# A recurrence on 64 x 64 quarters of the TensorE array

## What is computed

```
def step(S, inp):                       # for every token, every head
    r_t, w_t, k_t, v_t, kk_t, a_t = inp
    sa = jnp.einsum('bhij,bhj->bhi', S, -kk_t)
    S = S * w_t + sa[..., None] * (kk_t * a_t) + v_t[..., None] * k_t
    return S, jnp.einsum('bhij,bhj->bhi', S, r_t)
```

## Time and profile before

| | us |
|---|---|
| median of 3 runs | 1198.92 |
| range of the runs | 1193.13 to 1202.80 |
| the profiled execution | 1198.65 |
| its span | 1196.9 |
| TensorE, products, busy | 1139.4 |
| VectorE busy | 626.6 |
| ScalarE busy | 337.0 |
| recurrence, first product of round 0 | 568.11 |
| first products of rounds 1, 2 and 3 | 604.61, 636.68, 664.82 |
| last product of the inverse of round 3, start | 692.05 |

### The profile page before, as it was taken

The page is one execution under the profiler, slowest core; times in us unless marked ns, Lnnn a source line. Parts: engine busy times, 40 slices in busy tenths (PEclk is TensorE's granted clock), DMA queues, the critical chain, the costliest instruction groups (busy, mean ns, idle before and its releaser), DMA issues.

```text
span 1196.9 us, 21721 instructions
## 1 busy us (share of the span) xinstructions
PE 1139.4 (95%) x8994; PEld 1116.0 (93%) x8994; DVE 626.6 (52%) x1075; ACT 337.0 (28%) x496; POOL 40.7 (3%) x57
## 2 busy tenths in 40 slices
PE   6999999999999997999898999999999999999996
PEld 6999999999999997998787889989999999999996
DVE  5533343333345875889767616785343443344446
ACT  5321222111213433521234343442122221122221
POOL 0000000000000000210221100000000000000001
PEclk9999999999999988999799998899999999999998
DMA  6313232223222211332501002203233232323222
GB/s 223 113 55 105 89 102 74 88 88 100 76 95 79 74 50 53 77 89 76 41 1 36 1 1 73 57 33 106 80 99 104 70 105 71 106 71 105 70 71 75
DMA packets 35391, 92.23 MB, mean 77 GB/s; under 512 B 10368, under 2 KB 12928, under 8 KB 35200
## 3 DMA queue, kind: packets, MB, share of 16 engines
q1 hardware_dynamic: 34320, 88.78, 23.9%
q10 hardware_dynamic: 1008, 2.56, 0.6%
HBM read 88.05 MB, written 3.28 MB: 76 GB/s over the span
## 4 chain that ended last, share of the span: by engine, by line
PE 81%; DVE 12%; ACT 3%; issue 3%; DMA 1%; DVEq 0%; SPq 0%; ACTq 0%
PE ps L306 71%; DVE wl L289 1%; PE ps L1131 1%; DVE mixf L984 1%; PE ps L1137 1%; PE ps L1138 1%; PE ps L367 1%; DVE a L447 1%; ACT wh L284 1%; DVE tb L676 1%; PE ps L376 1%; DMA x<-in_x 1%; DVE xx L1310 1%; DVE mixf L985 1%; PE ps L1573 1%
## 5 line engine op out<-in xcount | busy, mean ns | idle before, releaser
L306 PE MATMUL ps<-xh,wh 128*128 128x272 f32 x1840 | 404.2, 293 | 22.7 <-DVE wl L289 8.8
L306 PE MATMUL ps<-xh,wl 128*128 128x272 f32 x1840 | 400.7, 291 | 0.0
L306 PE MATMUL ps<-xl,wh 128*128 128x272 f32 x1840 | 399.7, 290 | 0.0
L306 PEld LDWEIGHTS ps<-xh,wh 128*128 128x128 f32 x1840 | 299.6, 191 | 25.2 <-DVE wl L289 15.0
L306 PEld LDWEIGHTS ps<-xl,wh 128*128 128x128 f32 x1840 | 299.7, 191 | 0.0
L306 PEld LDWEIGHTS ps<-xh,wl 128*128 128x128 f32 x1840 | 297.9, 191 | 0.0
L284 ACT ACTIVATE wh<-raw 128x1024 fp32r<-128x1024 f32 (+1 forms) x163 | 167.7, 1032 | 319.5 <-PE ps L306 201.2
L289 DVE TENSOR_TENSOR wl<-raw,wh 128x1024 fp32r<-128x1024 f32 (+1 forms) x163 | 192.5, 1202 | 43.6 <-ACT wh L284 43.3
L306 PE MATMUL ps<-hh,wh 128*128 128x272 f32 x704 | 156.8, 289 | 0.0
L306 PE MATMUL ps<-hh,wl 128*128 128x272 f32 x704 | 155.8, 288 | 0.0
L306 PE MATMUL ps<-hl,wh 128*128 128x272 f32 x704 | 155.6, 288 | 0.0
(11 more groups left out here) (311 smaller groups left out, 850.5 us busy)
## 6 DMA issues: line engine op xcount, KB each, us to landing
raw<-in_w_gu SPq DMA_DIRECT2D x88, 512.0 KB, 3.7
raw<-in_w_d SPq DMA_DIRECT2D x32, 512.0 KB, 3.6
raw<-in_w_in SPq DMA_DIRECT2D x19, 512.0 KB, 3.5
raw<-in_w_d SPq DMA_DIRECT2D x16, 384.0 KB, 3.0
raw<-in_w_out SPq DMA_DIRECT2D x8, 512.0 KB, 3.6
out_y<-x SPq DMA_DIRECT2D x16, 136.0 KB, 1.7
con<-in_con ACTq DMA_DIRECT2D x1, 1158.5 KB, 5.1
x<-in_x ACTq DMA_DIRECT2D x4, 272.0 KB, 5.6
```

What stands on the lines that cost most here:

```text
L306: last = pe.matmul(out[:, n], left[:, s, j], right[:, j, n * H:n * H + H], start=first and opens and j == order[0], stop=final and closes ...
```

## The change

The inverse's matrices become 128 rows by 64 columns: the rows of chunk c keep their partitions, and the columns of both chunks share the same 64. Each 128 x 128 product of steps 2 to 12 becomes two products of 64 x 64, one for each c, on rows hp[c] and output partitions hp[c]. The transposes of step 2 become products with the identity. Line 1157 becomes two 64 x 64 products, on output partitions rows(c). The evictions of steps 2 to 12 have half the columns. VectorE's masks of step 1 are ordered anew: `nib` in two instructions of 64 partitions, one addition and one mask for both p instead of two each, `akb` in two of 64 partitions, `rbk` as before but behind both of `akb`. Step 2 waits for one count of `tt1` for both p. The mask and level tables in `con` shrink from 9 x 128 to 64 + 128 + 6 x 64 columns.

```diff
--- before.py
+++ after.py
@@ -66,7 +66,7 @@
 
 CCOL = {}
 _n = 0
-for _name, _k in (("ident", P), ("ones", P), ("hb", P), ("mask", 3 * P), ("lev", 6 * P), ("scan", N), ("cnt", 32),
+for _name, _k in (("ident", P), ("ones", P), ("hb", P), ("mask", C + P), ("lev", 6 * C), ("scan", N), ("cnt", 32),
                   ("wcol", 2), ("eps", 3), ("smask", 64), ("slev", 64), ("bsel", 8), ("idc", 64)):
     CCOL[_name] = _n
     _n += _k
@@ -88,12 +88,12 @@
     c[:, CCOL["ident"]:][:, :P] = s == t
     c[:, CCOL["ones"]:][:, :P] = 1
     c[:, CCOL["hb"]:][:, :P] = s // C == t // C
-    c[:, CCOL["mask"]:][:, :P] = (s // C == t // C) & (s < t)
-    c[:, CCOL["mask"] + P:][:, :P] = (s // C != t // C) & (s % C < t % C)
-    c[:, CCOL["mask"] + 2 * P:][:, :P] = s % C <= t % C
+    c[:, CCOL["mask"]:][:, :C] = s % C < t[:, :C]
+    c[:, CCOL["mask"] + C:][:, :P] = s % C <= t % C
     for n, b in enumerate(LEVELS):
-        near = (s // (2 * b) == t // (2 * b)) & (s // b != t // b)
-        c[:, CCOL["lev"] + n * P:][:, :P] = near & (s < t if n == 0 else s > t) | (s == t)
+        r, q = s % C, t[:, :C]
+        near = (r // (2 * b) == q // (2 * b)) & (r // b != q // b)
+        c[:, CCOL["lev"] + n * C:][:, :C] = near & (r < q if n == 0 else r > q) | (r == q)
     col = np.arange(N)
     start = np.where(col < NP_, col % C == 0, (col - NP_) % NT == 0)
     c[:, CCOL["scan"]:][:, :N] = 1 - start
@@ -201,15 +201,15 @@
 
         spots["wkv"] = W0
         bv = at("wkv", "bv", [2, 2, 3, P])
-        nib = at("wkv", "nib", [2, 2, P])
-        akb = at("wkv", "akb", [2, 2, P])
+        nib = at("wkv", "nib", [2, 2, C])
+        akb = at("wkv", "akb", [2, 2, C])
         rbk = at("wkv", "rbk", [2, 2, 2, P])
         rhs = at("wkv", "rhs", [2, P])
         assert spots["wkv"] <= LO
         spots["wkv"] = LO + 8 * N
-        tt_ = at("wkv", "tt", [2, 2, 2, P])
-        tf = at("wkv", "tf", [2, 2, P])
-        xx = at("wkv", "xx", [2, 2, P])
+        tt_ = at("wkv", "tt", [2, 2, 2, C])
+        tf = at("wkv", "tf", [2, 2, C])
+        xx = at("wkv", "xx", [2, 2, C])
         sfin = at("wkv", "sfin", [2, C])
         assert spots["wkv"] <= UB
         spots["wkv"] = UB
@@ -1121,21 +1121,27 @@
                     continue
                 elif s == 2:
                     b = job(p)
-                    pe.wait_ge(S("tt1"), 2 * t + p + 1)
+                    pe.wait_ge(S("tt1"), t + 1)
                     for h in range(2):
-                        last = pe.transpose(b[:, P * h:P * h + P], tt_[:, p, 1, h], ident)
+                        for c in range(2):
+                            last = pe.matmul(b[hp[c], C * h:C * h + C], tt_[hp[c], p, 1, h], ident[hp[c], C * c:C * c + C],
+                                             start=True, stop=True)
                 elif s % 2:
                     pe.wait_ge(S(f"r{s - 1}"), 2 * t + p + 1)
                     b = job(p)
                     for h in range(2):
-                        last = pe.matmul(b[:, P * h:P * h + P], nib[:, p, h], tt_[:, p, 0, h], start=True, stop=True)
+                        for c in range(2):
+                            last = pe.matmul(b[hp[c], C * h:C * h + C], nib[hp[c], p, h], tt_[hp[c], p, 0, h], start=True, stop=True)
                 else:
                     pe.wait_ge(S(f"r{s - 1}"), 2 * t + p + 1)
                     b = job(p)
                     for h in range(2):
                         if s < 12:
-                            pe.matmul(b[:, P * h:P * h + P], tt_[:, p, 1, h], xx[:, p, h], start=True, stop=True)
-                        last = pe.matmul(b[:, 256 + P * h:256 + P * h + P], xx[:, p, h], tt_[:, p, 1, h], start=True, stop=True)
+                            for c in range(2):
+                                pe.matmul(b[hp[c], C * h:C * h + C], tt_[hp[c], p, 1, h], xx[hp[c], p, h], start=True, stop=True)
+                        for c in range(2):
+                            last = pe.matmul(b[hp[c], P + C * h:P + C * h + C], xx[hp[c], p, h], tt_[hp[c], p, 1, h],
+                                             start=True, stop=True)
                 last.then_inc(S("job"), 1)
             if s == 1:
                 b = [job(h) for h in range(2)]
@@ -1154,8 +1160,9 @@
                     pe.wait_ge(S("r0"), 2 * t + p + 1)
                     for h in range(2):
                         k = P * p + C * h
-                        last = pe.matmul(ps[:, 4 + t % 2, k:k + C], akb[:, p, h], bv[:, t % 2, p, 2, C * h:C * h + C],
-                                         start=k == 0, stop=t == 0, skip_group_check=True)
+                        for c in range(2):
+                            last = pe.matmul(ps[rows(c), 4 + t % 2, k:k + C], akb[hp[c], p, h], bv[hp[c], t % 2, p, 2, C * h:C * h + C],
+                                             start=k == 0, stop=t == 0, skip_group_check=True)
                 if t == 0:
                     last.then_inc(S("c_injob"), 1)
 
@@ -1186,7 +1193,7 @@
                     pe.wait_ge(S("r12"), 2 * t + p + 1)
                     for h in range(2):
                         q = P * p + C * h
-                        last = pe.matmul(ps[rows(c), 4 + k, 256 + q:256 + q + C], tf[rows(c), p, h, cols(c)],
+                        last = pe.matmul(ps[rows(c), 4 + k, 256 + q:256 + q + C], tf[rows(c), p, h],
                                          rhs[rows(c), p, C * h:C * h + C], start=True, stop=True)
                 last.then_inc(S("c_ujob"), 1)
             elif hop in ("s0", "s1"):
@@ -1228,11 +1235,11 @@
                 if s == 0:
                     act.activation(bv[:, t % 2, p].rearrange("p a b -> p (a b)"), done(p)[:, 0:3 * P], ACT.Copy).then_inc(S("r0"), 1)
                 if s == 2:
-                    act.activation(tt_[:, p, 0], done(p)[:, 0:2 * P].rearrange(HC, h=2), ACT.Copy).then_inc(S("r2"), 1)
+                    act.activation(tt_[:, p, 0], done(p)[:, 0:P].rearrange(HC, h=2), ACT.Copy).then_inc(S("r2"), 1)
                 if s in (4, 6, 8, 10):
-                    act.activation(tt_[:, p].rearrange("p k h c -> p (k h c)"), done(p), ACT.Copy).then_inc(S(f"r{s}"), 1)
+                    act.activation(tt_[:, p].rearrange("p k h c -> p (k h c)"), done(p)[:, 0:2 * P], ACT.Copy).then_inc(S(f"r{s}"), 1)
                 if s == 12:
-                    act.activation(tf[:, p], done(p)[:, 256:512].rearrange(HC, h=2), ACT.Copy).then_inc(S("r12"), 1)
+                    act.activation(tf[:, p], done(p)[:, P:2 * P].rearrange(HC, h=2), ACT.Copy).then_inc(S("r12"), 1)
 
         yc = ar[:, :, 0, :]
 
@@ -1289,26 +1296,34 @@
                 def part(h):
                     return done(h).rearrange(quads, i=2, c=2, w=2)
 
-                def mask(n):
-                    return C_("mask", P, n * P).rearrange(HC, h=2).unsqueeze(1).to_broadcast([P, 2, 2, C])
+                def own(c, kind):
+
+                    two = ps[hp[c if kind == "b" else 1 - c], 2 * (place(("r", t, 1)) % 2):2 * (place(("r", t, 1)) % 2) + 2]
+                    return two.rearrange("p h (i c w k) -> p h i c w k", i=2, c=2, w=2)[:, :, :, c, 0]
+
+                hik = "p i h k -> p h i k"
+                strict = C_("mask", C).unsqueeze(1).unsqueeze(1)
+                upto = C_("mask", P, C).rearrange(HC, h=2).unsqueeze(1).to_broadcast([P, 2, 2, C])
+                wait_job(dve, t, s, 1)
+                for c in range(2):
+                    dve.tensor_tensor(nib[hp[c]].rearrange(hik), own(c, "b"), strict[hp[c]].to_broadcast([64, 2, 2, C]), MUL).then_inc(S("near"), 1)
+                four = "p i h k -> p (i h) k"
+                dve.wait_ge(S("near"), 2 * t + 2)
+                dve.tensor_tensor(nib[:].rearrange(four), nib[:].rearrange(four), C_("idc", C).unsqueeze(1).to_broadcast([P, 4, C]), ADD
+                                  ).then_inc(S("unit"), 1)
+                dve.wait_ge(S("unit"), t + 1)
+                dve.tensor_tensor(tt_[:, :, 1], nib[:], C_("lev", C).unsqueeze(1).unsqueeze(1).to_broadcast([P, 2, 2, C]), MUL).then_inc(S("tt1"), 1)
+                for c in range(2):
+                    r = hp[1 - c]
+                    dve.tensor_tensor(akb[r].rearrange(hik), own(c, "k"), strict[r].to_broadcast([64, 2, 2, C]), MUL).then_inc(S("ak"), 1)
                 for h in range(2):
-                    dve.tensor_tensor(nib[:, :, h].rearrange(ick, c=2), part(h)[:, :, :, 0], mask(0), MUL).then_inc(S("near"), 1)
-                idb = ident.unsqueeze(1).to_broadcast([P, 2, P])
-                for p in range(2):
-                    dve.wait_ge(S("near"), 2 * t + 2)
-                    dve.tensor_tensor(nib[:, p], nib[:, p], idb, ADD).then_inc(S("unit"), 1)
-                for p in range(2):
-                    dve.wait_ge(S("unit"), 2 * t + p + 1)
-                    dve.tensor_tensor(tt_[:, p, 1], nib[:, p], C_("lev").unsqueeze(1).to_broadcast([P, 2, P]), MUL).then_inc(S("tt1"), 1)
-                for h in range(2):
```

(7 more changed lines are left out.)

## The result

| | before | changed |
|---|---|---|
| median of 20 executions each | 1203.89 us | 1196.49 us |
| their range | 1193.13 to 1210.77 | 1180.74 to 1202.12 |
| ratio | | 0.991 (0.9885 to 0.9939) |

The change makes the kernel 0.9% faster; 1.3% was forecast (1182.6 against 1198.65). The median lies above the forecast's own range (1176 to 1187) and just under the top of the wide one (1175 to 1197). The kernel before is 5 us longer in this set than in the prediction's three runs; by the ratio, 10.5 us were gained where 16 were forecast. A second set, on another chip, gave 1208.4 for before and 1198.68 for the changed kernel, ratio 0.9927 (0.9898 to 0.9956).

The account below looks back on a forecast made before the run. TensorE's streamed products of line 306 hold 71% of the span, untouched; in the recurrence TensorE's queue carries every loss to the end. 1198.65 less 15.3 (recurrence) and 0.7 (constants) gives 1182.6 us; own range 1176 to 1187, wide 1175 to 1197.

Parts of the forecast that it names:

- the clock in its windows no lower: Recurrence, profile after: TensorE's granted clock would not fall below the 0.67, 0.80 and 0.93 of three windows before.
- a rival at 0.18: Recurrence: TensorE's granted clock falls; partly, 1186 to 1205 us, chance 0.12; through most of the stretch, 1212 us, 0.06.
- The price of the clock: Recurrence: an extra microsecond spent at the low clock costs about 0.5 us; 32 us more would cancel the gain.
- Records 0.030 us apart: Inverse's products, steps 2 to 12: 64 x 64 records follow each other at 0.030 us, full ones at 0.111.
- The rival by which the quarters take turns: Inverse's products: quarters writing to one bank don't overlap, 0.058 us a record; 1194.6 us, no measurable change; chance 0.12.
- The quiet level 2.03: One odd and one even step without other queued work: 2.03 us against 3.19, now a chain of latency.
- The recurrence 113 to 115 us long: The whole stretch of four rounds, as the profile after would show it; 15.3 us were to be saved there.
- A change of tile shape 0.16: TensorE's hand-overs between full and 64-column loads: 0.16 us late each, three more a round, 0.5 us a round.
- Round 3, 5.1 us: Last round of the recurrence: saves 5.1 us, 2.6 of it behind step 7, where the taps end.
- Rounds 1 and 2, 3.4 each: Recurrence: each saves 3.4 us, 2.5 of it on steps up to 7 and 0.9 behind, where VectorE's work is queued.
- VectorE binds everywhere: Recurrence: every level has taps or other work queued; the whole gains some 10 us, 1188.5 us; chance 0.15.
- The constants, 0.7: Kernel start: the smaller table's transfer saves 0.7 us, between 0 and 1.3.

Follow-up runs that it names:

- full products with more waits: Kernel before with the second head's products of steps 3 to 12 left out, so TensorE waits on a full array: ratio 0.9919, 1198.1 us.
- short taps: Convolution taps 6 and up on 64 of 512 prompt columns: changed kernel 0.9865, 1189.0 us; kernel before 0.9975, 1203.8 us.
- warmed kernels: Changed kernel plus unread TensorE products ahead of its waits: ratio 0.9894; in more places 0.9902; as quarter products 0.9922; with state updates moved later 0.9862.

## Why the prediction was wrong

**The step that failed** is the last word of the list of what would be right, "the clock in its windows no lower", and behind it the sum, which took the clock's part at nothing and left it to a rival at 0.18, of which 0.12 was for a partial fall. That rival came true in part: 0.013 of mean clock, by the line some 10 us. The reason given against it ("the clock came back within ten microseconds in which TensorE was busy half the time") was one place of one trace. The prediction had seen that the new levels leave TensorE idle for a third of their time, and had even named one low place behind a wait of 2.77 us; what it lacked was to put the clock into the sum as a term. Of the two causes it named, waiting is borne out, since full products with more waits lost clock too. "A quarter of the array in each record" is not: unread quarter products brought clock back, though it isn't excluded that they bring less.

**The price of the clock** was too high for the changed kernel, about 0.5 for each microsecond at 1.2 GHz, where its runs give 0.28 to 0.32; for the kernel before, with 0.37 to 0.45, it was nearer. Part of such a level is VectorE's and ScalarE's: all 32 and 40 evictions of a kind take 0.38 and about 0.29 us, whatever TensorE's clock. With its own price the prediction would have taken 12 us for the 24 us more of the profiled execution, where the line gives 7.7; too high a price and too small a gain (below) would have hidden each other.

**The rest of the sum held**, and was rather small.
- Records 0.030 us apart: 0.027, and 8 loads take 0.31 us where 0.35 to 0.45 was written. The rival by which the quarters take turns is refuted. The Trainium skill ("TensorEngine Tiling (Array Packing)", Restrictions and Gotchas) says that different row tiles can't access the same PSUM bank at the same time; for two on disjoint partitions, on diagonal quarters, the trace shows no cost of it.
- The quiet level 2.03: 2.11 (2.01 from step 7 to 9). Evictions 0.29 and 0.38: the same. The sum took 1.05 for such a level, though 3.19 - 2.03 is 1.16; it measured 1.08, so the slip did no harm.
- The recurrence 113 to 115 us long: 114.9, but 121.9 in the other profiled execution. The first figure is no sign that the sum was right, for it was reached at a lower clock than before's.
- A change of tile shape 0.16: from four loads at 668.35 the next was due at 668.47 and came at 668.61, 0.14.
- Round 3, 5.1 us: 5.6 at full clock, with short taps on both sides.
- Rounds 1 and 2, 3.4 each: 4.2 and 3.6 in the profiled execution, at a lower clock than before. VectorE bound them less than was taken. It was busy 19.56 of 27 us in round 1 and 19.20 of 23 in round 2 (72 and 83%), not over 85; it ends last only where updates, a split of weights or of y stand behind the taps. The rival "VectorE binds everywhere" gave the wrong extent. VectorE's whole part is the 5 to 7 us of the short taps, which the prediction had as lost gain behind step 7 of rounds 1 and 2.
- The constants, 0.7: the square of the input starts at 17.15 and not 17.69, after a wait of 3.52 and not 4.06. It is 0.54 at that place.

```profile
17.15 0.66 ACT L436 ACTIVATE a<-x 128x544 f32<-128x544 f32 x1 [3.52 <-DMA dwbd<-in_dw]
```

So the sum at equal clock was 16 and is about 21 by the line through the executions, 17.7 in the recurrence between two profiled ones of equal lost clock (the second with its updates moved and unread work added). What makes the difference between these two figures is open. So is how much of the 10 us is caused by the clock: round 3 shows 2 to 3 of them directly. By the ratios the warmed kernels got back 0.6 to 4 us for 0.007 to 0.013 of clock, with unread work to be paid from it, and no single one of these steps is outside its interval.

## What to carry to other kernels

When a change cuts TensorE's work in a stretch and leaves a chain of evictions and waits, put the granted clock into the sum as a term: read it in windows before the change, count the idle time that the change adds, and price it by executions of one kernel at different clocks, here 7.7 us for each 0.01 of mean clock in the changed kernel and 9 to 11 in the one before. Two remedies were tried here, and only together did they come out of the noise of one of the two sets: to move other engines' work out of the way of the chain, and to give TensorE something harmless to do ahead of its long waits. More of the second brought nothing more. And compare kernels at equal clock before judging the arithmetic of a change.

## What was not expected of the hardware

- 64 x 64 products on the two diagonal quarters, writing to one bank on different partitions, have records 0.027 us apart; one quarter alone takes 0.058 and a full product 0.111.
- Records for one quarter start before earlier ones for the other (line 1163 ahead of line 1142 above). The order of a timeline is not the program's there.
- Unread quarter products bring clock back (0.960 beside 0.967 of before), as full ones of the same duration do (0.961 beside 0.965), where the kernel without them has 0.951 beside 0.965.
- The 20 executions of the first set of the changed kernel range over 0.945 to 0.969 of mean clock and 1180.7 to 1202.1 us, and the two go together; a single profile of such a kernel says little on a change of 1%.
